# x turned by the host, modulation sums by accumulating VectorE operations, and two pairs of column tiles at once over all eight PSUM banks

## What is computed

```
cond = silu(c)                        # 1024
mod  = cond @ w_ada + b_ada           # 9 x 1024: shift, scale, gate of each of the 3 sub-layers
h = rms_norm(x, g_ffn1) * (1 + sc1) + sh1
x = x + 0.5 * gt1 * ((silu(h @ w1_a) * (h @ w3_a)) @ w2_a)      # d_ff = 2816
h = rms_norm(x, g_mix) * (1 + sc2) + sh2
x = x + gt2 * mixer(h)                # short convolution, a linear state space, gates, projections
h = rms_norm(x, g_ffn2) * (1 + sc3) + sh3
x = x + 0.5 * gt3 * ((silu(h @ w1_b) * (h @ w3_b)) @ w2_b)
out = rms_norm(x, g_final)
```

## Time and profile before

| | us |
|---|---|
| time, median of 3 runs | 2113.22 |
| lowest and highest | 2112.83, 2114.67 |
| profiled execution: span | 2111.0 |
| profiled execution: own time | not given apart from the span; the median is 2.2 above the span |
| TensorE busy | 2066.9 |
| GpSimd busy | 1405.3 |
| VectorE busy | 1367.0 |
| ScalarE busy | 744.7 |

### The profile page before, as it was taken

The page is one execution under the profiler, slowest core; times in us unless marked ns, Lnnn a source line. Parts: engine busy times, 40 slices in busy tenths (PEclk is TensorE's granted clock), DMA queues, the critical chain, the costliest instruction groups (busy, mean ns, idle before and its releaser), DMA issues.

```text
span 2111.0 us, 26148 instructions
## 1 busy us (share of the span) xinstructions
PE 2066.9 (98%) x9462; PEld 1695.1 (80%) x9462; DVE 1367.0 (65%) x1555; ACT 744.7 (35%) x1126; POOL 1405.3 (67%) x936
## 2 busy tenths in 40 slices
PE   7999999999999999999999999999999999999998
PEld 5778888888887778888888888887888888888887
DVE  6957868787778796877874654338537272635556
ACT  5633333333333453333333420116323333333334
POOL 1566878878785276856666655544858787778860
PEclk8999999999999999999999999999999999999999
DMA  8233251524232323233334444311111222111212
GB/s 301 60 115 105 67 174 41 155 85 120 90 110 65 123 83 96 80 107 97 91 93 153 161 158 147 110 50 40 53 47 41 60 61 60 50 51 50 70 42 80
DMA packets 220777, 197.41 MB, mean 94 GB/s; under 512 B 17028, under 2 KB 185136, under 8 KB 219504
## 3 DMA queue, kind: packets, MB, share of 16 engines
q1 hardware_dynamic: 196016, 154.42, 24.0%
q10 hardware_dynamic: 24640, 41.40, 6.0%
HBM read 169.45 MB, written 25.17 MB: 92 GB/s over the span
## 4 chain that ended last, share of the span: by engine, by line
PE 82%; DVE 8%; ACT 2%; issue 2%; DMA 2%; POOL 1%; ACTq 1%; SPq 0%; DVEq 0%; POOLq 0%
PE unit_d L1475 10%; PE unit_b L1475 10%; PE unit_b L1192 9%; PE unit_c L1475 7%; PE unit_a L1475 7%; PE unit_a L1192 6%; PE unit_a L1518 4%; PE unit_b L1518 4%; PE unit_b L1050 3%; PE unit_a L1050 2%; PE unit_d L1518 2%; PE unit_c L1518 2%; PE unit_d L1050 2%; PE unit_c L1050 2%; DMA ada_first<-in_w_ada 1%
## 5 line engine op out<-in xcount | busy, mean ns | idle before, releaser
L943 POOL TENSOR_TENSOR w_low<-raw,w_high 128x512 fp32r<-128x512 f32 x200 | 277.1, 1386 | 124.7 <-ACT w_high L1858 114.0
L1858 ACT ACTIVATE w_high<-raw 128x512 fp32r<-128x512 f32 x200 | 124.9, 630 | 294.2 <-PE unit_b L1475 117.7
L972 POOL TENSOR_TENSOR w_low<-raw,w_high 128x512 fp32r<-128x512 f32 x112 | 175.1, 1563 | 58.4 <-ACT w_high L1906 50.9
L894 POOL TENSOR_TENSOR w_low<-raw,w_high 128x512 fp32r<-128x512 f32 x80 | 119.1, 1488 | 111.1 <-ACT w_high L2068 107.2
L943 POOL TENSOR_TENSOR w_low<-w_mixed,w_high 128x512 fp32r<-128x512 f32 x76 | 105.5, 1388 | 37.7 <-ACT w_high L1858 33.5
L861 POOL TENSOR_TENSOR w_high<-raw,ones 128x512 fp32r<-128x512 f32 x44 | 59.4, 1349 | 98.1 <-PE unit_b L1050 33.4
L913 POOL TENSOR_TENSOR w_low<-raw,w_high 128x512 fp32r<-128x512 f32 x32 | 55.0, 1727 | 104.7 <-ACT w_high L1815 104.7
L2068 ACT ACTIVATE w_high<-raw 128x512 fp32r<-128x512 f32 x100 | 62.3, 630 | 163.2 <-PE unit_b L1192 108.2
L1906 ACT ACTIVATE w_high<-raw 128x512 fp32r<-128x512 f32 x112 | 67.8, 625 | 129.9 <-POOL raw L976 64.0
L1893 ACT ACTIVATE fg_high<-fg_two 128x1024 fp32r<-128x1024 f32 x56 | 59.4, 1061 | 145.8 <-PE unit_b L1518 45.7
L2763 DVE TENSOR_TENSOR fg_high<-fg_two,fg_high 128x1024 fp32r<-128x1024 f32 x56 | 95.7, 1710 | 0.0
(11 more groups left out here) (590 smaller groups left out, 6374.0 us busy)
## 6 DMA issues: line engine op xcount, KB each, us to landing
raw<-in_w_a SPq DMA_DIRECT2D x66, 512.0 KB, 4.4
raw<-in_w_b SPq DMA_DIRECT2D x66, 512.0 KB, 3.9
ada_ring<-in_w_ada SPq DMA_DIRECT2D x112, 256.0 KB, 3.0
raw<-in_w_in SPq DMA_DIRECT2D x44, 512.0 KB, 3.8
ada_first<-in_w_ada SPq DMA_DIRECT2D x8, 1024.0 KB, 20.6
sg_kept<-s ACTq DMA_DIRECT2D x16, 512.0 KB, 2.7
s<-sg_kept ACTq DMA_DIRECT2D x16, 512.0 KB, 3.3
x_rows<-in_x SPq DMA_DIRECT2D x8, 512.0 KB, 6.9
```

The costliest lines, as they stand in the source:

```text
L894: pool.tensor_tensor(low_, mixer_plain(q, slots), high.bitcast(F32), ALU.subtract).then_inc(mixer.operand_low, 1)
L943: pool.tensor_tensor(low_, weight_plain(PRODUCTS[q][0], slots, mixed), high.bitcast(F32), ALU.subtract).then_inc(f.operand_low, 1)
L972: pool.tensor_tensor(low_, block_unit(here, u), high.bitcast(F32), ALU.subtract).then_inc(f.operand_low, 1)
L1858: act.activation(operand((here.ring[n] + q) % 4)[0], weight_plain(PRODUCTS[q][0], slots, mixed_of(here, n)), ACT.Copy).then_inc(f.operand_ ...
```

## The change

1. **The host lays inputs out.** x comes turned, in two halves of the tokens, [2, 128, 8, 512]; `w_ada` transposed, 72 tiles of 128 outputs x 1024; w1, w3 and w_in by column tiles, [tile, 128, 8, 128], so that a partition's run is 4 KB; the small tables as one [128, 164] array `vt`. TensorE's turning of x and of the tables and their copies go.
2. **`cond` is a row on all partitions.** c is loaded as one row, spread by two TensorE products with a row of `ones`, and Silu writes `cond` [128, 1024].
3. **Modulation sums run along the row.** One `scalar_tensor_tensor` with `accum_out` gives one column of 128 outputs. For the first norm: 16 of them over 1024, from a ring of three pairs of tiles (8 transfers of 1 MB), inside the norm. For the rest: 14 windows of eight pieces of 128x512, each piece one operation that reads the condition from a PSUM bank (`cond_copy`, a copy from SBUF; from the third window on the half of `cond` needed is loaded again from memory) and writes the product over its piece. `ada_tiles` on TensorE and `ada_copy` on ScalarE go.
4. **The first norm goes k by k**, both halves of the tokens in turn, with `rstd_first` in SBUF. TensorE takes both tiles of w1 and of w3 at once, over all eight banks (`first_whole_tiles`); the second halves of the four weight tiles have their high and low parts in `w_behind`.
5. **Orders change with it.** Windows 0 and 1 are both summed within matrix 1; before, block 0 was summed ahead of matrix 0. ScalarE's and VectorE's lists between the tiles and matrix 0 are put in another order.

```diff
+            def first_whole_tiles(f):
+                pe.wait_ge(cond_ready, 1)
+                for n, (k, half) in enumerate(FIRST_STEPS):
+                    t = slice(HALF * half, HALF * half + HALF)
+                    xh, xl = (x[:, k % HK, :] for x in norm_operand(0, half, k // HK))
+                    pe.wait_ge(h_ready, n + 1)
+                    for u in range(4):
+                        if half == 0 and k % HK == 0:
+                            pe.wait_ge(f.operand_low, 4 * (k // HK) + u + 1)
...
+                        wh, wl = (x[:, k % HK, :] for x in first_operand(4 * (k // HK) + u))
+                        for part, (w, x) in enumerate(((wh, xh), (wh, xl), (wl, xh))):
+                            last = pe.matmul(unit[u][:, t], w, x, start=(k == 0 and part == 0),
+                                             stop=(k == KD - 1 and part == 2))
...
-            ada_columns(ada_first_sum, ada_first, 16 * P, ada_loaded)
-            root(0, 0)
...
+                def column_sum(k, s_):
+                    slot = ada_pairs[k % RING_PAIRS]
+                    if s_ == 0:
+                        dve.wait_ge(ada_loaded[k % RING_PAIRS], 16 * (k // RING_PAIRS + 1))
+                    dve.scalar_tensor_tensor(out=slot[:, s_, :], in0=slot[:, s_, :], scalar=1.0, in1=cond[:, :], op0=mul, op1=mul,
+                                             accum_out=acc_first[:, 2 * k + s_:2 * k + s_ + 1]).then_inc(ada_summed, 1)
...
+                column_sum(0, 0)
+                column_sum(0, 1)
+                first_root(0)
+                scaled(0)
+                low(0)
+                first_root(1)
+                scaled(1)
+                column_sum(1, 0)
+                low(1)
+                column_sum(1, 1)
+                for k in range(1, KD):
+                    scaled(2 * k)
+                    scaled(2 * k + 1)
+                    if k + 1 < KD:
+                        column_sum(k + 1, 0)
+                    low(2 * k)
+                    if k + 1 < KD:
+                        column_sum(k + 1, 1)
+                    low(2 * k + 1)
...
-                    if k == 0:
-                        if b > 0:
-                            dve.wait_ge(ada_copied, b)
-                        dve.tensor_scalar(to, ada_ring[r][:, :], by, None, mul).then_inc(ada_used, 1)
-                    else:
-                        dve.wait_ge(ada_used, p)
-                        dve.scalar_tensor_tensor(out=to, in0=ada_ring[r][:, :], scalar=by, in1=to,
-                                                 op0=mul, op1=add).then_inc(ada_used, 1)
+                    n = window_columns(b) + k
+                    to = acc_half[:, k:k + 1] if h else mod[:, n:n + 1]
+                    dve.scalar_tensor_tensor(out=ada_ring[r][:, :], in0=ada_ring[r][:, :], scalar=1.0, in1=cond_bank(b),
+                                             op0=mul, op1=mul, accum_out=to).then_inc(ada_used, 1)
...
+                    if more:
+                        cond_copy(0, (f.evacuated, 5))
+                        cond_copy(1, (f.evacuated, 5))
+                        ada_pieces(0, 0, 3)
                     dve.wait_ge(f.first_copied, here.matrix[n] + 1)
                     out_of(1, 2, u2, u2, bank(w, 1))
                     if more:
-                        ada_pieces(1, 0, 2, (f.evacuated, 5))
+                        ada_pieces(0, 3, 3)
...
                     if more:
-                        ada_pieces(1, 2, 3)
+                        ada_pieces(0, 6, 2)
+                        ada_pieces(1, 0, 1)
...
                     if more:
                         mod_add(0)
+                        ada_pieces(1, 1, 1)
...
                         gated_block(5, 0, 2, 0, 0, bank(w, 0))
                         if more:
-                            ada_pieces(1, 5, 3)
+                            ada_pieces(1, 2, 3)
                         low_block(1, 1, 1)
                         out_of(6, 6, bank(w, 2), u2, bank(w, 2), 1)
                         gated_block(7, 6, 3, 0, 1, bank(w, 2))
                         if block is not None:
                             mod_add(block)
+                        if more:
+                            ada_pieces(1, 5, 3)
+                            mod_add(1)
+                            own.then(half_gate(0, 0))
                         low_block(2, 0, 0)
                         low_block(3, 0, 1)
                         out_of(8, 7, bank(w, 3), u2, bank(w, 3), 1)
                         gated_block(9, 8, 4, 1, 0, bank(w, 3))
```

More of the change, by code:

```diff
@@ L85, with window_columns, window_half @@
 PAIRED = (FT - 2) // 4
-BLOCKS = (NMOD - 2 * KD) // 4
+WINDOWS = 2 * (NMOD - 2 * KD) // KD
 RING_ADA = 3
+RING_PAIRS = 3
+def window_columns(b):
+    return 2 * KD + KD * (0 if b < 2 else b - 1 if b < 8 else b - 7)
+def window_half(b):
+    return int(b == 1 or b >= 8)
+FIRST_STEPS = [(k, half) for k in range(KD) for half in range(2)]
 DOWN_PRODUCTS = (("a11", 0, True), ("s1", 1, True), ("a12", 0, False), ("s4", 1, False), ("s3", 0, True), ("s2", 1, True),
@@ L757, in chunk @@
                             load_matrix(after, n, e)
-                for z in range(2 if with_ada else 0, 4):
-                    if not with_ada:
+                if not with_ada:
+                    for z in range(4):
                         sp.wait_ge(slab_split, 2 * (ffn_at(f).slab + z - 3))
-                    first(z)
+                        first(z)
                 here = Chunk(1, f.n)
@@ L1115, in statistics_begun @@
                 pe.matmul(unit[C_][:, t], ones[:, :], s0[:, t], start=n == 1, stop=False).then_inc(sq_used, 1)
-            take(D_, J // 2)
-            for part, (k0, k1) in enumerate(FIRST_MOD):
-                pe.wait_ge(ada_summed, part + 1)
-                for t in [*range(k0, k1), *range(KD + k0, KD + k1)]:
-                    last = pe.matmul(unit[D_][:, HALF * part + t:HALF * part + t + 1],
-                                     ada_first_sum[:, t * P:(t + 1) * P], ones[:, 0:1], start=True, stop=True)
-                last.then_inc(ada_full, 1)
             def mixer_whole(here, between):
@@ L1440, in matrix @@
                 elif n == 0 and here.first:
-                    for u in (A_, B_):
-                        take(u, units[u] + 1)
+                    take(A_, units[A_] + 1)
                 else:
@@ L1759, in norm @@
                 root(0)
-                if n == 0:
-                    root(1)
-                    for o in range(4):
-                        part, z = divmod(o, 2)
-                        act.wait_ge(first_ffn.w_loaded[z], 16)
-                        act.activation(operand(o)[0], raw[:, z, part * HK:(part + 1) * HK, :], ACT.Copy).then_inc(
-                            first_ffn.first_high, 1)
                 for step in range(2 * KD):
@@ L1772, in norm @@
                         square_end(n, step // 4, 1)
-                    if n > 0 and step == 6:
+                    if step == 6:
                         root(1)
@@ L1777, in norm @@
                     act.wait_ge(xr_done, 2 * KD * n + step + 1)
-                    for part, (k0, _) in enumerate(FIRST_MOD):
-                        if n == 0 and step == k0:
-                            act.wait_ge(mod_done, part + 1)
                     own.then(act.activation(tile, tile, ACT.Identity, scale=scale[n][:, m:m + 1],
@@ L1880, in first_copy @@
                     act.wait_ge(f.operand_used, here.op[n] + 1)
+                    if f.n == 0 and here.first and n == 2:
+                        act.wait_ge(cond_kept_done, 16)
                     if here.blocks and n == 3:
@@ L1913, in block_down @@
                         block_unit_high(here, u)
-                        if u == (1 if here.first else 0) and 3 in here.mod_block:
-                            ada_copy(here.mod_block[3])
                 def matrix(here, n):
@@ L2521, in _ @@
+            def mod_add(b):
+                n = window_columns(b)
+                dve.wait_ge(ada_used, KD * b + KD)
+                by = acc_half[:, :] if window_half(b) else vt[:, B_ADA + n:B_ADA + n + KD]
+                own.then(dve.tensor_tensor(mod[:, n:n + KD], mod[:, n:n + KD], by, add))
+            lr, li = (vt[:, AR + KP * part:AR + KP * part + KP] for part in range(2))
             Q = [x[:, :] for x in qs]
```

553 lines of the change are left out of this document (301 added, 252 removed).

## The result

The changed kernel takes **2118.15 us** (median of 10 runs, 2115.08 to 2122.33), the kernel before 2113.02 beside it (10 runs, 2112.09 to 2115.58). The ratio is 1.0023, 95% interval 1.0014 to 1.0032: **slower by 0.23%**, 5 us, where 15.5 us less were forecast. In the profiled executions the span grows from 2111.0 to 2116.4.

The account below looks back on a forecast made before the run. The prediction took TensorE, busy for 98% of the span, to bound the kernel. Its terms, -9.2 - 13.4 + 7.1 = -15.5 us, gave 2097.7 us, with a range for 8 in 10 of 2086 to 2109.

Parts of the forecast that it names:

- the second term: TensorE loses the one-column products of ada_tiles in 14 blocks, 0.96 us each, counted in full: -13.4 us.
- the start: From the kernel's beginning through first norm and matrix 0: matrix 1 starts at 110.5 instead of 119.7, -9.2 us.
- the new wait: In first_down, TensorE's second tile waits for gating behind windows 0 and 1 in VectorE's queue: +7.1 us.
- the wait of 2.8: In matrix 0, ahead of the fifth product, which was put at 26 us after the norm's end.
- Pieces and copies: Later windows: pieces stay at 0.75 us, the added copy of 0.67 is hidden; +4 at most if not.
- Layout: Weights laid out in tiles, 4 KB runs instead of 512 bytes: raw loads are hidden by splits, costed at nothing.
- Half-rate sums: First norm: the accumulating sum of 128x1024 with two SBUF tensors takes 2.35 us; 2112.4 us in all, chance 0.10.
- VectorE keeps up: First norm: GpSimd's ops miss VectorE's, norm ends at 71, ring refills hide most of the wait; 2087.7 us, chance 0.15.
- Slower by dear pieces: Later windows: accumulating pieces of 128x512 cost about 1.4 us instead of 0.75; 2141 us in all, chance 0.08.
- signs of failure: The prediction fails if the norm's end is far from 76, or windows' pieces start to hold TensorE in each chunk.

Follow-up runs that it names:

- experiment 2: The kernel before without the one-column products of ada_tiles in all 14 blocks, later modulation values not computed: 0.9989.
- experiment 1: The changed kernel with eight one-column products put back as dummies in each of the 12 later matrices that have a window: 1.0029 of the kernel before.
- experiment 3: The changed kernel with GpSimd's four raw sums of block_down in the first block cut to 16 columns: 0.9966 of the kernel before.
- experiment 5: The changed kernel with matrix 1's last gatings ahead of window 1's last pieces: 0.9997 of the kernel before.
- experiment 9: The kernel before with only w1, w3 and w_in laid out by the host in tiles of 128 output columns: 1.0001.
- experiments 4, 12: The changed kernel with powers_and_turns moved: its first step behind matrix 2's third sum, 1.0006; all steps behind the last chunk's folds, 1.0043 (ratios to the kernel before).
- experiment 14: The changed kernel with gatings first in matrix 1 and two of block_down's four raw sums on VectorE instead of GpSimd: 1.0032 of the kernel before.

## Why the prediction was wrong

**The step that failed** is the second term: "All of it lies in a stretch where TensorE has no idle time, so it counts in full". It doesn't follow. TensorE without idle time says that no other engine needs longer, not that the others need less by any margin. GpSimd needed almost as long in one stage of the five of a chunk, `block_down`, and the average over a window that mixed it with matrices didn't show that. Of 13.4 us 2.3 count in the kernel before (experiment 2), and putting 11 back costs about 1 (experiment 1); with GpSimd's sums cut, `block_down` takes 38.1 and 12 us come back (experiment 3).

The span was to be 2095.5 us and is 2116.4, 20.9 more. Of these 10.5 are the growth of the four `block_down`s, 6.1 the last chunk, 2.3 the part of the 13.4 that the matrices up to there didn't give (they gave 11.1), 1.6 the start and 1.1 the new wait; behind the last chunk 0.7 come back.

**The start**, -9.2 forecast, measured -7.6. The marks hold: tiles steady from 41 (38 forecast), norm end 77.0 (76), second product 92.7 (91), matrix 1 at 112.1 (110.5). The norm is 1.0 late and the second product another 0.7. Behind the 7 us wait the lower clock cost 3.0 where 0.5 was allowed (the product took 5.26 instead of 2.72, the next three 2.84 to 2.92). Against that, the wait of 2.8 that the working had ahead of the fifth product never came: from the second product to matrix 1 TensorE is busy for 19.36 of 19.40 us. So two errors of the working nearly cancel, and that this mark comes within 1.6 is in part luck.

**The new wait**, +7.1 forecast, 8.2 measured: 5.3 of waiting (5.2 forecast) and 2.9 for the clock (1.9 forecast; two products of 5.26 and 3.07 instead of 2.72). Place, releaser and length were right; experiment 5 shows that it is the pieces ahead of the gating and not the gate itself.

**Pieces and copies** in the later chunks: right. A piece takes 0.69 with 0.08 for the accumulator's read beside the next one (0.75 forecast), the four matrices of a chunk take 76.2 us, 28 products of 2.72 without a gap.

**Layout**: right (experiment 9).

**The last chunk**, 6.1 us, had no term at all. `powers_and_turns` isn't touched by the diff; it lies between sums that TensorE waits for, and had just enough cover. That its small steps are the stall is shown (experiments 4, 12), that they slow beside GpSimd is what the rows show. The removal of the products is enough to bring 3.5 us of it (experiment 2); what closes GpSimd's pause of 1.33 us, in which they ran fast before, was not isolated.

**Rivals.** Half-rate sums: a sum of 128x1024 with two SBUF tensors took 1.21, not 2.35. The halving that the Trainium skill states for this form (Vector Engine (DVE) Microarchitecture Reference, Points that are easy to get wrong) is not seen: 1.21 is what a plain `tensor_tensor` of that size takes here. VectorE keeps up: no, the norm ends at 77.0 and not at 71. Slower by dear pieces: they weren't dear (0.69). The sign of that rival came true by a mechanism that no rival had. The price of the start and of the wait was inside the bounds, and the range missed because its floor and ceiling both let the 13.4 count. Neither of the two signs of failure that the prediction named came true, the norm's end far from 76 or pieces that hold TensorE in each chunk; the step that failed had no sign of its own.

## What to carry to other kernels

A busy engine without gaps is a bound only until its work is cut; before pricing a cut, take the windows stage by stage and ask of each other engine how much less than the stage it needs, handshakes and contention included (here 33.9 us of GpSimd in 38.6 of `block_down`, with a lead of four operands). Where two engines slow each other, a shift of 1 us can also change which operations meet, and so how long a list takes (here 39.8 or 41.8). Take the saved work out of the old kernel alone, or put dummies back into the new one: two runs told which term was worth next to nothing. A saving on the busiest engine is worth what the next one lets through, so it is made together with relief for that one. And work moved to another engine costs more than it gives when it waits there behind other work and the first engine needs its result (experiment 14).

## What was unexpected of the hardware

Very short VectorE operations suffer most, for their length, beside GpSimd: 128x16 with SBUF inputs takes 0.17 us in GpSimd's pause and 1.16 beside its operations of 1.3 us, close to a whole one. GpSimd's sum of 128x1024 takes 2.38 in one place and 3.47 in another. The Trainium skill (SBUF — State Buffer, Who interferes with whom) says that VectorE with two SBUF inputs contends with GpSimd's reads over a shared pair of ports, and that this is an exclusive lock. These rows agree, 0.17 against 1.16: the short operation waits for nearly a whole one of GpSimd and isn't just slowed in proportion.

The accumulating form was as fast as the plain one: 128x1024 in 1.21 and 128x512 in 0.69, and the accumulator's read of 0.08 overlaps the next operation (67.36 in the rows of the norm's end).
